# Column sums of the latents' squares moved between the products of chunk 7's dense groups, and the last dense group moved behind the values

## The chip, the cores and the metric

One core of a Trainium2 chip runs the kernel. The metric is the device time of one execution in microseconds (us); 3 runs of the kernel before were timed.

## What is computed

Two layers of a hybrid decoder, for a prompt of 1024 tokens and 8 sequences of 4 new tokens (NT = 1056 tokens in all, width 1024). Each layer projects the normed input with one matrix, runs an mLSTM over chunks and a latent attention (MLA) beside it, joins both in an output projection, and then adds a convolutional feed-forward part and a gated embedding. The part that matters here, cut from the reference:

```python
h = rmsnorm(x, lw['norm_mix'])
z = h @ lw['w_in']
qm, km, vm, om, im, fm, cq, ckv, kr = jnp.split(z, splits, axis=-1)
...
hm, C, n, m = mlstm_chunkwise(qm, km, vm, ig, lf, C0, n0, m0)
hm = rmsnorm(hm.astype(x.dtype), lw['m_norm']).reshape(B, T, M_WIDTH) * jax.nn.sigmoid(om)
lat = jnp.concatenate([rmsnorm(ckv, lw['mla_kv_norm']), rope(kr, pos)], axis=-1)
qa = (rmsnorm(cq, lw['mla_q_norm']) @ lw['mla_w_uq']).reshape(B, T, A_HEADS, A_NOPE + A_ROPE)
```

`rmsnorm` divides by the root of the mean of squares over the latent's width (384 for `cq`, 256 for `ckv`). The sums of these squares, one number per token and latent, are what the change moves.

## The kernel before, in words

The kernel works on transposed tensors: features on the 128 partitions, tokens along the row. A row of 1056 tokens is cut into NC = 3 column chunks of 352. Float32 products are made of three matmuls of rounded halves (`product3`, lines 223 to 225: high x high, high x low, low x high). Each layer is a series of phases; in a phase every engine has its own program, the engines signal one another through semaphores, and a phase ends with a barrier of all engines once its own waits are through.

The phase of the change is `mix_projection` (line 557 on), which runs once per layer. It computes the matrix product with `w_in` as a list of **dense groups**, `GROUPS`. A group is one tile of 128 output features for one column chunk: 8 steps over the input width of 3 matmuls each, 24 matmuls of 128x352, into one PSUM bank. ScalarE evacuates each group (`evacuate`). The last four weight jobs hold 24 groups (`MIXED` and on); these are dealt out to the 8 mLSTM chunks of 128 tokens, three to a chunk, so that they cover the chunk's steps on the other engines. TensorE's loop (line 1035) reads for each chunk c:

```python
dense(MIXED + 3 * c)
spread(c)
dense(MIXED + 3 * c + 1)
scores(c)
dense(MIXED + 3 * c + 2)
values(c)
```

`spread` brings decay rows and the transposed keys to PSUM, VectorE and ScalarE make decay matrices of them (`decays`), `scores` multiplies keys and queries (L988), VectorE multiplies both (`decayed_scores`, L747), and `values` (L1001, L1002, L1008) makes the numerators and the state's update, from which VectorE computes the chunk's heads and the new state (`outputs`). ScalarE squares the heads (`squares`, L886). The last groups are output gates (`og`): ScalarE puts them into one of two buffers `og_staging` (L843), and SyncE stores each to DRAM (`out_gate`, L628). SyncE's list is fixed: behind the last store of a gate comes the store of the final state (L652), and then its waits for every store, which the end of the phase needs.

In chunks 4 to 6 ScalarE squares the latents' tiles and VectorE adds them up (`latent_squares`), into `core.norm` for `cq` and `mem.sqk` (in the profile kv_squares) for `ckv`. After the loop TensorE waits for the last evacuation and makes for each of the two rows of squares 9 column sums: each takes a tile of 128 tokens as stationary operand and a column of ones as moving one (L1046), into a PSUM bank of its own. ScalarE takes the root (L931), VectorE the inverse (L813, the tile `mla_rt`), and TensorE turns the inverses of `cq` into rows with 9 transposes (L1051), in banks 0 to 2. This is the end of the phase. The next one, `mla_prepare`, begins with SyncE's loads (L1122, L1123), VectorE's scaling of `cq` (L1329) and the parts of `cq` that TensorE waits for.

## Time and profile before

| | |
|---|---|
| median of 3 runs | 3104.38 us (3102.88 to 3104.58) |
| the profiled execution's own time | 3111.33 us |
| its span in the profile | 3109.5 us |
| TensorE busy | 96% of the span |
| VectorE busy | 51% |
| ScalarE busy | 36% |
| mean granted clock of TensorE | 0.978 |

The span is what the profile covers of one execution; times in rows are microseconds from its start. The page's first part lists busy shares; the timeline lists instructions in order, with the idle time before one and who ended it. A granted clock of 1.00 is 2.4 GHz, one of 0.50 is 1.2 GHz. Each sum, and each product of the scores and values, is recorded as two passes, so 9 sums appear as 18 matmuls. The transposes are recorded as one.

### The profile page before, as it was taken

Reading aid. Unit: us, or ns where it says so; the run is one execution under the profiler, and the core shown is the slowest. Engines: PE = TensorE matmul, PEld = TensorE weight load, DVE = VectorE, ACT = ScalarE, POOL = GpSimd, SP = SyncE. Lnnn points to the kernel's source line nnn. Section 1 sums busy time; section 2 is a strip of 40 time slices with the busy share of each in tenths; the row PEclk is TensorE's granted clock in tenths of the full one; section 3 lists DMA queues with packets and bytes.
Section 4 is the critical chain, followed back from the end, with each engine's and each line's share of the span. In section 5 each row is a group of like instructions: output and inputs, shape, how many; then the busy total and the mean of one; then the engine's idle time right before and its main releaser. Section 6 shows DMA issues by size and latency. Waiting matters only on the chain. (4 is left out here: it accounts for less than half of the span.)

```text
span 3109.5 us, 46695 instructions
## 1 busy us (share of the span) xinstructions
PE 2984.0 (96%) x19219; PEld 2809.4 (90%) x19219; DVE 1581.0 (51%) x2696; ACT 1134.9 (36%) x2148; POOL 142.8 (5%) x260
## 2 busy tenths in 40 slices
PE   6999989999999999999989999999999999999997
PEld 5998755899999999998989887559999999999997
DVE  5233634565454555457661346445654555445665
ACT  6223423443333323335452333334533223333353
POOL 0000300000000000000000004000000000000000
PEclk9999889999999999999999989999999999999999
DMA  3101243421111111112221021533211111111121
GB/s 129 42 28 45 94 145 113 151 73 55 41 50 47 41 55 41 55 47 82 89 71 42 14 94 57 175 99 137 73 55 41 41 55 43 53 41 41 47 96 70
DMA packets 70742, 215.40 MB, mean 69 GB/s; under 512 B 6522, under 2 KB 43386, under 8 KB 54146
## 3 DMA queue, kind: packets, MB, share of 16 engines
q1 hardware_dynamic: 70530, 212.42, 19.8%
q8 instruction: 152, 2.49, 0.3%
q14 instruction: 60, 0.49, 0.1%
HBM read 193.52 MB, written 18.87 MB: 68 GB/s over the span
## 5 line engine op out<-in xcount | busy, mean ns | idle before, releaser
L223 PE MATMUL psum<-h_chunk,out_weight_parts 128*128 128x352 f32 x2112 | 681.5, 323 | 0.0
L224 PE MATMUL psum<-h_chunk,out_weight_parts 128*128 128x352 f32 x2112 | 677.1, 321 | 0.0
L225 PE MATMUL psum<-h_chunk,out_weight_parts 128*128 128x352 f32 x2112 | 676.4, 320 | 0.0
L2233 DVE SCALAR_TENSOR_TENSOR conv_sum<-u_padded,vectors,conv_sum 128x1024 f32<-128x1024 f32 x176 | 226.3, 1286 | 540.1 <-ACT conv_sum L2085 537.0
L224 PEld LDWEIGHTS psum<-h_chunk,out_weight_parts 128*128 128x128 f32 x2112 | 396.8, 188 | 0.0
L223 PEld LDWEIGHTS psum<-h_chunk,out_weight_parts 128*128 128x128 f32 x2112 | 396.2, 188 | 0.0
L225 PEld LDWEIGHTS psum<-h_chunk,out_weight_parts 128*128 128x128 f32 x2112 | 395.9, 187 | 0.0
L223 PE MATMUL psum<-g_parts,out_weight_parts 128*128 128x352 f32 x960 | 309.3, 322 | 0.0
L224 PE MATMUL psum<-g_parts,out_weight_parts 128*128 128x352 f32 x960 | 309.0, 322 | 0.0
L225 PE MATMUL psum<-g_parts,out_weight_parts 128*128 128x352 f32 x960 | 308.8, 322 | 0.0
L2259 DVE TENSOR_TENSOR x<-x,psum 128x352 f32<-128x352 f32 x528 | 254.9, 520 | 94.4 <-PE psum L225 94.0
L2081 ACT ACTIVATE u_padded<-psum 128x352 f32<-128x352 f32 (+1 forms) x264 | 119.8, 454 | 494.1 <-PE psum L225 494.1
L217 DVE TENSOR_TENSOR out_weight_parts<-out_weight_stage,out_weight_parts 128x2048 fp32r<-128x2048 f32 x80 | 183.3, 2292 | 62.6 <-ACT out_weight_parts L211 62.6
L223 PE MATMUL psum<-h_high,mix_weight_parts 128*128 128x352 f32 x576 | 192.9, 335 | 13.1 <-DVE mix_weight_parts L217 10.1
L2097 ACT ACTIVATE g_parts<-conv_sum 128x1056 fp32r<-128x1056 f32 x40 | 43.4, 1086 | 417.5 <-PE psum L225 345.3
L224 PE MATMUL psum<-h_low,mix_weight_parts 128*128 128x352 f32 x576 | 187.5, 325 | 0.0
L225 PE MATMUL psum<-h_high,mix_weight_parts 128*128 128x352 f32 x576 | 187.4, 325 | 0.0
L225 PEld LDWEIGHTS psum<-g_parts,out_weight_parts 128*128 128x128 f32 x960 | 180.6, 188 | 0.0
L224 PEld LDWEIGHTS psum<-g_parts,out_weight_parts 128*128 128x128 f32 x960 | 180.3, 188 | 0.0
L223 PEld LDWEIGHTS psum<-g_parts,out_weight_parts 128*128 128x128 f32 x960 | 180.3, 188 | 0.0
L2085 ACT ACTIVATE conv_sum<-psum,vectors 128x352 f32<-128x352 f32 x264 | 170.5, 646 | 0.0
L211 ACT ACTIVATE out_weight_parts<-out_weight_stage 128x2048 fp32r<-128x2048 f32 x80 | 152.7, 1908 | 6.1 <-PEq L142 6.0
(356 smaller groups left out, 5502.0 us busy)
## 6 DMA issues: line engine op xcount, KB each, us to landing
out_weight_stage<-w_up_dram SPq DMA_DIRECT2D x44, 1024.0 KB, 4.7
out_weight_stage<-w_down_dram SPq DMA_DIRECT2D x22, 1024.0 KB, 4.7
mix_weight_stage<-w_in_dram SPq DMA_DIRECT2D x18, 1024.0 KB, 4.9
pages<-cache_dram SPq DMA_DIRECT2D x64, 288.0 KB, 4.4
out_weight_stage<-w_out_dram SPq DMA_DIRECT2D x16, 1024.0 KB, 5.9
out_weight_stage<-w_gate_dram SPq DMA_DIRECT2D x16, 1024.0 KB, 4.8
pages<-cache_dram SPq DMA_DIRECT2D x64, 160.0 KB, 2.6
x<-x_in_dram SPq DMA_DIRECT2D x6, 1408.0 KB, 11.1
```

The costliest lines, as they stand in the source:

```text
L211: act.activation(dst[:, 0, 0:width], self.stage[:, staged, 0:width], ACT.Copy).then_inc(self.ph["hi_made"], 1)
L217: dve.tensor_tensor(dst[:, 1, 0:width], self.stage[:, slot % self.stages, 0:width], dst[:, 0, 0:width].bitcast(F32), ALU.subtract).then_in ...
L223: pe.matmul(out, lhs[0], rhs[0], start=first, stop=False)
L224: pe.matmul(out, lhs[0], rhs[1], start=False, stop=False)
L225: return pe.matmul(out, lhs[1], rhs[0], start=False, stop=last)
L2081: act.activation(u[:, q, 2 + c * CH:2 + c * CH + n], src[:, 0:n], ACT.Copy)
L2085: op = act.activation(t[:, q, chunk(c)], src, ACT.Identity, bias=bias, scale=w2)
L2097: act.activation(dst, t[:, 1, :], ACT.Copy).then_inc(ph["ghi_made"], 1)
L2233: dve.scalar_tensor_tensor(t[:, q, 0:SEQ], row[:, tap:tap + SEQ], w, t[:, q, 0:SEQ], ALU.mult, ALU.add).then_inc(ph["conv_step"], 1)
L2259: dve.tensor_tensor(X[:, k, chunk(c)], X[:, k, chunk(c)], ps[:, (6 + n) % 8, 0:CH], ALU.add).then_inc(ph["x_made"], 1)
```

## The change

In chunk 7 the first dense group gets the 9 column sums of `core.norm`, the second those of `mem.sqk`. One sum stands behind each of the first 7 steps of the group, two behind its end. The last dense group moves behind values(7), and waits until the roots are taken, since its bank is the one in which the sums now lie (`SUM_GROUP`, the group that used the bank before). ScalarE takes the roots behind the evacuation of chunk 7's second group, then squares the heads, then evacuates the last group. VectorE makes the inverse ahead of outputs(7). Roots and inverses lie in unused columns of `mem.cwc` instead of a tile of their own. The transposes stay at the end, behind the last evacuation.

```diff
--- before.py
+++ after.py
@@ -608,6 +608,7 @@
         ring = WeightRing(None, ph, "mix_projection", stages=1, stage=mem.mix_stage, parts=mem.mix_parts, ready=ready)
         first_third = 1 if l else 0
         LATE = KX * (2 - first_third)
+        SUM_GROUP = len(GROUPS) - 4
         ps = core.psum
 
         def bank(g):
@@ -806,11 +807,12 @@
                 decayed_scores(c)
                 if 4 <= c < 7:
                     latent_squares(c)
+                if c == NCK - 1:
+                    dve.wait_ge(ph["rt_step"], 2)
+                    dve.reciprocal(mem.rt_inverse, mem.rt).then_inc(ph["rs_made"], 1)
                 outputs(c)
                 if c in (1, 3):
                     ring.lo(dve, 7 + c // 2, JW)
-            dve.wait_ge(ph["rt_step"], 2)
-            dve.reciprocal(mem.rt[:, 1], mem.rt[:, 0]).then_inc(ph["rs_made"], 1)
 
         @block.scalar
         def _(act):
@@ -924,17 +926,19 @@
                 if 4 <= c < 7:
                     latent_squares(c)
                 evacuate(MIXED + 3 * c + 1)
-                evacuate(MIXED + 3 * c + 2)
-                if c == NCK - 1:
-                    for i, d in enumerate((Q_RANK, KV_RANK)):
-                        act.wait_ge(ph["lsum_done"], i + 1)
-                        act.activation(mem.rt[:, 0, i, :], ps[:, i, 0:TT], ACT.Sqrt, bias=core.eps,
-                                       scale=1.0 / d).then_inc(ph["rt_step"], 1)
-                squares(c)
+                if c < NCK - 1:
+                    evacuate(MIXED + 3 * c + 2)
+                    squares(c)
+            for i, d in enumerate((Q_RANK, KV_RANK)):
+                act.wait_ge(ph["lsum_done"], 2)
+                act.activation(mem.rt[:, :, i], ps[:, bank(SUM_GROUP), TT * i:TT * (i + 1)], ACT.Sqrt,
+                               bias=core.eps, scale=1.0 / d).then_inc(ph["rt_step"], 1)
+            squares(NCK - 1)
+            evacuate(len(GROUPS) - 1)
 
         @block.tensor
         def _(pe):
-            def dense(g):
+            def dense(g, latent=None):
                 j, i, kind, t, c = GROUPS[g]
                 if g in START:
                     pe.wait_ge(ph["lo_made"], j + 1 - ready)
@@ -951,7 +955,12 @@
                         w = [W[:, q, k * 256 + i * P:k * 256 + (i + 1) * P] for q in range(2)]
                         x = [H(q, k, chunk(c)) for q in range(2)]
                         mm = product3(pe, ps[:, bank(g), 0:CH], w, x, k == 0, k == KX - 1)
+                    if latent is not None and k < KX - 1:
+                        latent_sum(latent, k)
                 mm.then_inc(ph["mm_done"], 1)
+                if latent is not None:
+                    for c in range(KX - 1, TT):
+                        latent_sum(latent, c)
 
             def gate_columns():
                 pe.wait_ge(ph["gate_act"], 6)
@@ -1008,6 +1017,16 @@
                     mm = pe.matmul(ps[part(h), B_UPD, (h // 2) * DV1:(h // 2 + 1) * DV1],
                                    kw[:, c % 2, h * 64:(h + 1) * 64], vTM[:, c, h, :], start=True, stop=True)
                 mm.then_inc(ph["upd_done"], 1)
+
+            def latent_sum(i, c):
+                if c == 0:
+                    pe.wait_ge(ph["lsq_added"], 2 + i)
+                    pe.wait_ge(ph["bank_free"], SUM_GROUP + 1)
+                n = TT * i + c
+                mm = pe.matmul(ps[:, bank(SUM_GROUP), n:n + 1], (core.norm, mem.sqk)[i][:, token_tile(c)],
+                               core.ones[:, 0:1], start=(n == 0), stop=True, skip_group_check=True)
+                if c == TT - 1:
+                    mm.then_inc(ph["lsum_done"], 1)
 
             if not ready:
                 pe.wait_ge(ph["lo_made"], 1)
@@ -1033,23 +1052,21 @@
             pe.wait_ge(ph["state_zeroed"], 3)
             pe.wait_ge(ph["cwc_made"], 2)
             for c in range(NCK):
-                dense(MIXED + 3 * c)
+                dense(MIXED + 3 * c, 0 if c == NCK - 1 else None)
                 spread(c)
-                dense(MIXED + 3 * c + 1)
+                dense(MIXED + 3 * c + 1, 1 if c == NCK - 1 else None)
                 scores(c)
-                dense(MIXED + 3 * c + 2)
-                values(c)
+                if c < NCK - 1:
+                    dense(MIXED + 3 * c + 2)
+                    values(c)
+            values(NCK - 1)
+            pe.wait_ge(ph["rt_step"], 2)
+            dense(len(GROUPS) - 1)
             pe.wait_ge(ph["bank_free"], len(GROUPS))
-            pe.wait_ge(ph["lsq_added"], 3)
-            for i, squares in enumerate((core.norm, mem.sqk)):
-                for c in range(TT):
-                    mm = pe.matmul(ps[:, i, c:c + 1], squares[:, token_tile(c)], core.ones[:, 0:1],
-                                   start=(c == 0), stop=True, skip_group_check=True)
-                mm.then_inc(ph["lsum_done"], 1)
             pe.wait_ge(ph["rs_made"], 1)
             for c in range(TT):
                 tr = pe.transpose(ps[:, c // 4, c % 4 * P:(c % 4 + 1) * P],
-                                  mem.rt[:, 1, 0, c:c + 1].to_broadcast([P, P]), core.ident)
+                                  mem.rt_inverse[:, c, 0:1].to_broadcast([P, P]), core.ident)
             tr.then_inc(ph["rows_done"], 1)
 
 
@@ -1069,7 +1086,7 @@
     krot = at(M_KROT, "k_rotated", [P, NT])
     cs = at(M_CS, "rope_cos_sin", [P, 2, NT])
     hrt = at(M_KROT + NT, "h_rms", [P, 2, 4 * TT])
-    rt, c0 = mem.rt, mem.c0
+    c0 = mem.c0
     og = at(M_KN, "og_all", [P, 4, NT])
     take = core.slab.bump(M_UQ + 4 * 768, M_CS)
     kw = take("ks_weighted", [NS, 256])
@@ -1207,7 +1224,7 @@
                 for c in range(TT):
                     out = ps[:, RB[1] + c // 4, c % 4 * P:(c % 4 + 1) * P] if c < TT - 1 else \
                         ps[:, TAIL[1][0], TAIL[1][1]:TAIL[1][1] + P]
-                    tr = pe.transpose(out, rt[:, 1, 1, c:c + 1].to_broadcast([P, P]), core.ident)
+                    tr = pe.transpose(out, mem.rt_inverse[:, c, 1:2].to_broadcast([P, P]), core.ident)
                 tr.then_inc(ph["rb_done"], 1)
 
             def numerators():
@@ -2790,7 +2807,6 @@
         self.sqt = at(M_QR + NT, "one_square", [P, NT])
         self.c0 = at(M_KN + 4 * NT, "state_sample", [P, DEC_BATCH, 2, DV1])
         self.uq = at(M_KN + 4 * NT + DEC_BATCH * 2 * DV1, "q_weight_stage", [P, 2, 768])
-        self.rt = at(M_KROT + NT + 72, "mla_rt", [P, 2, 2, TT])
         self.H = Halves(at(M_CATM, "h_high", [P, KX, NT], F32R), at(X_AT, "h_low", [P, KX, NT], F32R))
         self.mix_parts = at(M_KN, "mix_weight_parts", [P, 2, 2, JW], F32R)
         self.mix_stage = at(M_QR, "mix_weight_stage", [P, 1, JW])
@@ -2807,6 +2823,7 @@
         self.vTM = at(M_V, "m_v", [P, TT, M_HEADS, DV1])
         self.rows = at(M_ROWS, "m_rows", [64, NT])
         self.cwc = at(M_CWC, "m_columns", [P, TT, 96])
+        self.rt, self.rt_inverse = self.cwc[:, :, 4:6], self.cwc[:, :, 6:8]
         self.hS = at(M_HS, "m_h_sample", [P, M_HEADS, M_DV])
         self.ssq = at(M_SSQ, "m_ssq", [P, 4 * TT])
```

**TensorE, end of chunk 7's first dense group in layer 0.** L223 to L225 are one step of a group, L971 (L980 after) and L978 (L987 after) are `spread`. Before:

```order
L223 MATMUL psum<-h_high,mix_weight_parts 128x352
L224 MATMUL psum<-h_low,mix_weight_parts 128x352
L225 MATMUL psum<-h_high,mix_weight_parts 128x352
L971 MATMUL psum<-m_rows,constants 128x128 [waits h_made_0]
L971 MATMUL psum<-m_rows,constants 128x128 x7
L978 MATMUL psum<-constants,m_k 128x128 [waits state_made_0]
L978 MATMUL psum<-constants,m_k 128x128
```

With the change (L1026 is a sum; norm holds the squares of `cq`):

```order
L1026 MATMUL psum<-constants,norm 128x1
L223 MATMUL psum<-h_high,mix_weight_parts 128x352
L224 MATMUL psum<-h_low,mix_weight_parts 128x352
L225 MATMUL psum<-h_high,mix_weight_parts 128x352
L1026 MATMUL psum<-constants,norm 128x1 x2
L980 MATMUL psum<-m_rows,constants 128x128 [waits h_made_0]
L980 MATMUL psum<-m_rows,constants 128x128 x7
L987 MATMUL psum<-constants,m_k 128x128 [waits state_made_0]
```

The sums of `cq` stand singly behind the steps, the last two together behind the group. The second group reads in the same way, with kv_squares.

**TensorE, from chunk 7's scores to the end of the phase.** L988 (L997 after) are the scores, L1001, L1002 and L1008 (L1010, L1011 and L1017) the values. Before:

```order
L988 MATMUL psum<-m_q,mix_work 128x128 [waits kT_made_0,sd_made_0]
L988 MATMUL psum<-m_q,mix_work 128x128 x3
L223 MATMUL psum<-h_high,mix_weight_parts 128x352 [waits bank_free_0]
...
L1001 MATMUL psum<-m_v,mix_work 128x129 [waits sd_made_0,state_made_0,qa_made_0,dm_made_0]
L1002 MATMUL psum<-mix_work 128x129
...
L1008 MATMUL psum<-m_v,mix_work 64x129 x3
L1046 MATMUL psum<-constants,norm 128x1 [waits lsq_added_0,bank_free_0]
L1046 MATMUL psum<-constants,norm 128x1 x8
L1046 MATMUL psum<-constants,kv_squares 128x1 x9
L1051 MATMUL psum<-constants,mla_rt 128x128 [waits rs_made_0]
L1051 MATMUL psum<-constants,mla_rt 128x128 x8
```

With the change:

```order
L1026 MATMUL psum<-constants,kv_squares 128x1 x2
L997 MATMUL psum<-m_q,mix_work 128x128 [waits kT_made_0,sd_made_0]
L997 MATMUL psum<-m_q,mix_work 128x128 x3
L1010 MATMUL psum<-m_v,mix_work 128x129 [waits sd_made_0,state_made_0,qa_made_0,dm_made_0]
L1011 MATMUL psum<-mix_work 128x129
...
L1017 MATMUL psum<-m_v,mix_work 64x129 x3
L223 MATMUL psum<-h_high,mix_weight_parts 128x352 [waits bank_free_0,rt_step_0]
L224 MATMUL psum<-h_low,mix_weight_parts 128x352
L225 MATMUL psum<-h_high,mix_weight_parts 128x352
```

The values stand directly behind the scores, the last dense group behind the values and behind a wait for the roots (rt_step), and behind that group only the transposes are left.

**ScalarE, the end of the phase.** L843 (L845 after) evacuates an output gate, L877 (L879) is the decay exponential, L886 (L888) a square of the heads. Before:

```order
L877 ACTIVATE mix_work<-mix_work,m_columns 128x128 x3
L843 ACTIVATE og_staging<-psum 128x352 [waits og_stored_0,mm_done_0]
L843 ACTIVATE og_staging<-psum 128x352 [waits og_stored_1,mm_done_0]
L931 ACT_TABLE_LOAD
L931 ACTIVATE mla_rt<-psum,constants 128x9 [waits lsum_done_0] x2
L886 ACTIVATE mix_work,m_ssq<-m_v 128x128 [waits sq_step_0,h_made_0]
L886 ACTIVATE mix_work,m_ssq<-m_v 128x128 [waits sq_step_0] x3
```

With the change:

```order
L879 ACTIVATE mix_work<-mix_work,m_columns 128x128 x3
L845 ACTIVATE og_staging<-psum 128x352 [waits og_stored_0,mm_done_0]
L934 ACT_TABLE_LOAD
L934 ACTIVATE m_columns<-psum,constants 128x9 [waits lsum_done_0] x2
L888 ACTIVATE mix_work,m_ssq<-m_v 128x128 [waits sq_step_0,h_made_0]
L888 ACTIVATE mix_work,m_ssq<-m_v 128x128 [waits sq_step_0] x3
L845 ACTIVATE og_staging<-psum 128x352 [waits og_stored_1,mm_done_0]
```

The table load and the two roots stand ahead of the last evacuation instead of behind it, and so do the squares of the heads. SyncE's own order is as before: the last gate's store, then the state's.

## Rows read from the trace of the kernel before

**Rows 1.** The page: busy shares, and a group of weight loads (busy us, mean ns).

```profile
PE 2984.0 (96%) x19219; PEld 2809.4 (90%) x19219; DVE 1581.0 (51%) x2696; ACT 1134.9 (36%) x2148; POOL 142.8 (5%) x260
...
L224 PEld LDWEIGHTS psum<-h_chunk,out_weight_parts 128*128 128x128 f32 x2112 | 396.8, 188 | 0.0
```

**Rows 2.** Timeline, layer 0: start, duration, engine, line, operation, idle before.

```profile
303.32 0.72 PE L988 MATMUL psum<-m_q,mix_work 64*128 64x128 f32 x8
303.96 0.43 PE L223 MATMUL psum<-h_high,mix_weight_parts 128*128 128x352 f32 x1
...
307.94 0.39 PE L1001 MATMUL psum<-m_v,mix_work 128*128 128x129 f32 x2
...
311.77 3.28 PE L1046 MATMUL psum<-constants,norm 128*128 128x1 f32 x18
314.92 3.98 PE L1046 MATMUL psum<-constants,kv_squares 128*128 128x1 f32 x18
319.55 2.18 PE L1051 MATMUL psum<-constants,mla_rt 128*128 128x128 f32 x9 [0.66 <-DVE mla_rt L813]
```

**Rows 3.** Timeline, TensorE, layer 1, the same place.

```profile
1842.83 2.17 PE L1046 MATMUL psum<-constants,norm 128*128 128x1 f32 x18
1844.86 3.70 PE L1046 MATMUL psum<-constants,kv_squares 128*128 128x1 f32 x18
1849.22 2.18 PE L1051 MATMUL psum<-constants,mla_rt 128*128 128x128 f32 x9 [0.66 <-DVE mla_rt L813]
```

**Rows 4.** Timeline, ScalarE, layer 0.

```profile
318.93 0.27 ACT L931 ACTIVATE mla_rt<-psum,constants 128x9 f32<-128x9 f32 x1 [3.57 <-PE psum L1046]
...
320.61 0.19 ACT L886 ACTIVATION_READ_ACCUMULATOR mix_work<-m_v 128x1 f32 x1
```

**Rows 5.** Timeline, VectorE, layer 0.

```profile
304.08 0.76 DVE L747 TENSOR_TENSOR mix_work<-psum,mix_work 128x256 f32<-128x256 f32 x2 [3.33 <-PE psum L988]
...
311.96 0.76 DVE L763 TENSOR_TENSOR m_v<-psum,mix_work 128x256 f32<-128x256 f32 x2
...
319.23 0.27 DVE L813 RECIPROCAL mla_rt<-mla_rt 128x18 f32<-128x18 f32 x1 [5.12 <-ACT mla_rt L931]
```

**Rows 6.** Timeline, SyncE's transfers, layer 0, and one of layer 1.

```profile
308.63 0.32 SPq L628 DMA_DIRECT2D out_gate<-og_staging  x1
314.20 0.34 SPq L652 DMA_DIRECT2D state_p_out_dram<-mix_work  x1
322.69 0.33 SPq L1122 DMA_DIRECT2D rope_cos_sin<-cos_sin_dram  x1
323.07 0.43 SPq L1123 DMA_DIRECT2D og_all<-out_gate  x1
...
1852.76 0.33 SPq L1122 DMA_DIRECT2D rope_cos_sin<-cos_sin_dram  x1
```

**Rows 7.** Stretches: length, busy of each engine, granted clock (PEclk), DMA share, GB/s.

```profile
170.00:311.80 141.80, 141.80 (x940) 127.36 (x938) 48.60 (x127) 44.09 (x127) 0.00 (x0) 1.00 0.12 40
...
311.80:313.00 1.20, 1.20 (x12) 1.20 (x10) 1.07 (x5) 0.00 (x0) 0.00 (x0) 0.83 0.00 0
...
329.70:332.80 3.10, 3.08 (x11) 3.10 (x12) 3.10 (x5) 1.75 (x6) 0.54 (x1) 0.50 0.88 373
332.80:336.00 3.20, 3.20 (x21) 3.20 (x21) 2.51 (x7) 1.09 (x2) 1.91 (x3) 0.96 0.09 31
...
1845.00:1846.00 1.00, 1.00 (x7) 1.00 (x7) 0.17 (x1) 0.27 (x1) 0.00 (x0) 0.59 0.00 0
```

**Rows 8.** Timeline, TensorE, three sums between dense groups of the output projection.

```profile
606.38 0.32 PE L225 MATMUL psum<-heads_chunk,out_weight_parts 128*128 128x352 f32 x1
606.54 0.72 PE L2369 MATMUL psum<-constants,norm 128*128 128x1 f32 x6
...
607.37 0.32 PE L224 MATMUL psum<-heads_chunk,out_weight_parts 128*128 128x352 f32 x1
```

**Rows 9.** SyncE's own waits, 285 to 345 us: total, times, longest.

```profile
SPq L657 <- DMA state_p_out_dram<-mix_work: 1.8, 1, 1.8
```

## The prediction

> **What bounds the kernel now.** I read the page first. TensorE is busy for 96% of the span [rows 1], so the time can fall only where TensorE stands still or works slowly. The change touches one such place, the end of the mix projection, which comes once in each of the two layers. I then read TensorE's timeline there. In layer 0 the values of chunk 7 run from 307.94 to 311.77, then come the 18 column sums of squares (two passes each, so 36 matmul records), up to 318.90, a pause, and nine transposes up to 321.73 [rows 2]. In layer 1 the same places are 1842.83 (call the end of the values V), 1848.56 and 1851.40 [rows 3]. ScalarE and VectorE show that the chain is serial: sums, root (318.93), inverse (319.23), transposes (319.55) [rows 2, 4, 5]. SyncE issues its first transfer of the next phase at 322.69 and 1852.76 [rows 6]. So V to the next phase takes 10.92 us in layer 0 and 9.93 in layer 1. That is all that can be won, about 21 us in 3111.33. The difference of 1 us between the layers is the granted clock: it falls to the lower level (0.50, 1.2 GHz) early in the sums of layer 0 and late in those of layer 1 [rows 7].
>
> **The sums, moved between products.** No sum is removed; 36 (two layers of 18) stand elsewhere. The price of one alone between products of a dense group is not in the trace. The nearest place has three sums (six passes) between two dense groups: from the last product before (606.38) to the second after them (607.37) are 0.99 us, where two steps without sums take 0.32 [rows 8]. Thus three sums cost 0.67, one 0.22. The first load of weights of such a piece runs beside the product ahead, and what is then exposed is the second load and that of the next product, again two. I take 0.23 us per sum, 4.14 per layer. The lower bound is the 0.226 of layer 1's sums at the higher clock (2.03 us from 1842.83 to 1844.86 for nine), the upper the 0.41 of the nine that follow (3.70 us) [rows 3].
>
> That a load runs beside the product ahead is shown by the dense products: a load takes 188 ns by its mean [rows 1], yet they start every 0.16 us (606.38 to 606.54) [rows 8]. The Trainium skill (TensorE: Matmul & The Clock Gate, Part 3, The mechanism) says that weight loads overlap matmuls in flight only where the row groups differ, which these full loads do not. By that rule a single sum would expose three loads instead of two (its price is in the rivals). The rows speak against it.
>
> **A wait that appears.** Values(7) now stand directly behind scores(7). Before, the last dense group covered the multiplication of scores and decays on VectorE: the group began at 303.96, VectorE finished at 304.84 [rows 2, 5]. With a handover of 0.05 (319.50 to 319.55, inverse to transposes) TensorE waits 304.89 - 303.96 = 0.93 us. The decay exponentials are long done and cost nothing. What is behind this wait on the queue are values(7) and the last dense group, all of it on the path.
>
> **Edits that cost nothing.** The root moves on ScalarE behind the evacuation of the second dense group; its table load and two roots (0.27 us each) run while TensorE does the values (3.83 us), and the last dense group, which waits for them, comes later. The inverse (0.27 us) stands ahead of outputs(7), which wait for the values anyway. squares(7) start after the heads (312.72, that is 4.8 us behind the start of the values), take 1.6 us (319.20 to 320.80) and end 6.4 behind it; the last evacuation is due 3.83 + 3.98 (303.96 to 307.94) = 7.8 behind it [rows 2, 4, 5]. If that cover were gone, the squares' whole 1.6 us would stand ahead of the last evacuation and on the path. The strided place of the roots concerns 18 elements a row.
>
> **The end of the phase.** The last dense group ends its slots at E = V + 4.14 + 0.93 = V + 5.07. Now its evacuation and its store are late too. Before, the store was issued 0.69 us behind that point (308.63 - 307.94), and the state's store came at 314.20, far ahead of the end [rows 2, 6]. After the change both are queued on SyncE behind the last evacuation: og_staging at E + 0.69, the state 0.38 later (the distance of two issues, 322.69 to 323.07). SyncE must see the state land: 0.34 of issue and 1.8 of waiting [rows 6, 9]. This gives V + 5.07 + 0.69 + 0.38 + 2.14 = **V + 8.28**. TensorE's nine transposes wait for the same evacuation, start with the store's issue at about E + 0.7 and take 2.18 us even at the lower clock, so they end at V + 7.95 or earlier: **the state's landing is late next**, by 0.3 us at least. Before, the transposes, the phase's last work, ended at V + 9.96 (321.73) in layer 0 and V + 8.57 in layer 1. So 1.68 us and 0.29 us are won, 1.97 in all, if the clock stays up as before until V. The change may then bring 3111.33 - 1.97 = 3109.4 on the profiled execution, and 3102.4 on the median of the runs, which is 6.95 us below that execution; I make the sum on the difference and subtract it from the median.
>
> **The clock.** What the clock did before: behind the last dense product it stayed at 1.00 through the 3.83 us of the values alone of every chunk (its mean is 1.00 over 170.00 to 311.80, which holds all eight), but with sums behind the values it fell 4.7 us behind the end of the dense group (307.94) in layer 0 (inside 311.80 to 313.00, whose mean is 0.83, so at about 312.6) and 6.2 us behind it (V - 3.83 = 1839.00) in layer 1 (0.59 in 1845.00 to 1846.00, so about 1845.2), though TensorE was busy for 1.00 of that time [rows 7]. After the change the stretch without dense products between the second and the third dense group is two trailing sums 0.46, scores 0.64 (303.32 to 303.96), the wait 0.93 and the values 3.83 [rows 2]: 5.86 us. That lies between 4.7 and 6.2, and is emptier than the values alone. **I expect the clock to fall there in at least one of the layers.** It then stays low through the rest of the values and part of the last dense group. The price is bounded from below by the dense products at the lower clock at the next phase's start: 11 in the 3.10 us from 329.70, all at 0.50, where 0.16 each would be 1.8, a loss of 1.3 us [rows 7]. From above: the whole of the values (slower by the same 0.41/0.226 as the sums, 3.1 us more) and the whole last group (24 x 0.12 = 2.9), 6.0 us. As a fall can come anywhere in the values, I take 2.7 us, nearer the lower end because the clock was back at once after those 3.1 us of dense work (0.96 in the next 3.2), and 1.5 falls over the two layers: 4.0 us.
>
> The Trainium skill (TensorE: Matmul & The Clock Gate, table in "Why this matters for your kernels") warns of idle gaps between bursts of matmuls. By that rule nothing would happen here, since the engine idles for under 1 us, and the result would be that of the first rival. The rows of the sums, a fall at full busy time, say that idling is not needed.
>
> **Forecast: 3104.38 - 1.97 + 4.0 = 3106.4 us**, the likeliest case, chance 0.62; its own range is one fall at the low price to two falls at a higher one, 3103.8 to 3110. A measurement here can tell 0.2%, 6.2 us, from no change; so this is "no change".
>
> **Rivals.**
> - The clock holds in both layers: 3102.4 us. For it speaks that all chunks of the layer hold through their values [rows 7]; against it the 5.86 us. Chance 0.18.
> - The sums are dear when single. If their first load did not run beside the product ahead, three passes of 0.113 would be exposed, 0.34 us, and the two layers would lose 18 x 0.11 x 2 = 4.0 us: 3106.4 with the clock held; at the upper bound of 0.41 they lose 6.5, 3108.9. For it speaks that every piece changes between the two kinds of matmul; against it the 0.67 for three [rows 8]. Chance 0.07. This is the rule on row groups cited above.
> - **Slower than before by over 0.2%**: the clock falls right behind the scores and, with too little work in the slow values, does not come back until the last dense group is over, in both layers. At 6.0 us each this is 3102.4 + 12.0 = 3114.4. It decides for slower from 4.1 us per layer on (6.2 + 1.97 over two). Against it: the clock came back after 3.1 us of dense work. Chance 0.08.
> - The landing does not bind and the transposes run at the higher clock (twice as fast, 2.18 becomes 1.1): the phase ends at V + 6.9, 1.4 us earlier per layer, 3099.6 us. It needs a store that lands sooner than its like before. Chance 0.05.
> - That the change does not do what it says would be a wait of the first sum for squares or for the bank. The squares' additions end in chunk 6, and the bank was evacuated behind values(6), before the group starts: no wait, within the 0.05 above.
>
> **Range and chances.** The range takes the forecast's own, the clock held and dear sums: 3101.5 to 3110.5, and leaves out the two ends, under 0.15. Faster by over 0.2% (below 3098.2) has no mechanism here: 0.02. Slower by over 0.2%: the third rival and the tail of the first case, 0.09. Within: 0.89.
>
> **What would show it.** Single sums between products at steps of about 0.23 us; TensorE idle 0.9 us between scores and values for VectorE; the granted clock below 1.00 inside the last values and products of 0.29 us in the last group; SyncE's wait for state_p_out as the end of the phase, 8.3 us plus the fall's price behind the old V. The forecast is wrong if the clock is at 1.00 until the transposes, or if the steps at the sums are well above 0.3 us, or if the next phase starts later behind the landing than the 0.96 and 1.36 us that lay between the transposes and SyncE's first issue.

## The result, and the profile after

The change made the kernel slower: 3121.81 us (median of 5 runs, 3112.66 to 3124.23) against 3104.58 us before (5 runs in turn with them, 3102.88 to 3107.24). The ratio on record is 1.0049, with a 95% interval of 1.0039 to 1.006. The ratios in this document are those of the record, which aren't quotients of the medians (here 1.0055), and they leave out three executions of 5584, 5999 and 12777 us, of blocks_old_order, dummy_blocks and the kernel before. The result is outside the predicted range, and it is the sign of the third rival. The runs also lie wider apart than before, over 11.6 us instead of 4.4.

The profiled execution is the quickest of the five: 3112.66 us, span 3110.9 us. The page looks as before, with the same busy time of TensorE to 0.4 us [rows 1] and the same weight loads. (The profiled execution of before, 3111.33 us, was slower than all its timed runs; a second profile of it, below, has a span of 3099.7.)

```profile
PE 2984.4 (96%) x19219; PEld 2810.4 (90%) x19219; DVE 1580.2 (51%) x2696; ACT 1134.8 (36%) x2148; POOL 142.8 (5%) x260
...
L224 PEld LDWEIGHTS psum<-h_chunk,out_weight_parts 128*128 128x128 f32 x2112 | 396.8, 188 | 0.0
```

A busy share cannot show this change, because an engine at half its clock is as busy as one at full clock. The timeline does. TensorE in layer 0, the kernel after, in the order of time; these rows answer to [rows 2]:

```profile
293.55 0.32 PE L225 MATMUL psum<-h_high,mix_weight_parts 128*128 128x352 f32 x1
293.70 0.28 PE L1026 MATMUL psum<-constants,norm 128*128 128x1 f32 x2
293.84 0.41 PE L223 MATMUL psum<-h_high,mix_weight_parts 128*128 128x352 f32 x1
...
294.40 0.28 PE L1026 MATMUL psum<-constants,norm 128*128 128x1 f32 x2
...
302.22 0.42 PE L1026 MATMUL psum<-constants,kv_squares 128*128 128x1 f32 x2
...
303.53 0.42 PE L1026 MATMUL psum<-constants,kv_squares 128*128 128x1 f32 x2
...
309.53 1.22 PE L997 MATMUL psum<-m_q,mix_work 64*128 64x128 f32 x8
311.81 0.55 PE L1010 MATMUL psum<-m_v,mix_work 128*128 128x129 f32 x1 [1.06 <-DVE mix_work L748]
...
318.65 0.66 PE L223 MATMUL psum<-h_high,mix_weight_parts 128*128 128x352 f32 x1
...
324.40 1.20 PE L1068 MATMUL psum<-constants,m_columns 128*128 128x128 f32 x9 [0.55 <-ACT og_staging L845]
```

In the first group a step of three products and one sum takes 0.70 us (293.70 to 294.40), where a step without a sum takes 0.48: 0.22 for a sum. In the second group the same step takes 1.31 us (302.22 to 303.53). The wait for VectorE is there (1.06). The scores take 1.22 instead of 0.72, the values 311.81 to 318.65, which is 6.84 us instead of 3.83.

Stretches of the same place (length, busy of each engine, granted clock, DMA share, GB/s):

```profile
293.00:297.70 4.70, 4.70 (x37) 4.69 (x35) 0.99 (x3) 1.61 (x9) 0.00 (x0) 1.00 0.01 3
297.70:299.40 1.70, 1.70 (x18) 1.58 (x18) 0.58 (x1) 0.16 (x1) 0.00 (x0) 1.00 0.29 106
299.40:300.40 1.00, 1.00 (x8) 1.00 (x9) 0.94 (x4) 0.66 (x3) 0.00 (x0) 1.00 0.00 0
300.40:301.40 1.00, 1.00 (x6) 1.00 (x6) 0.51 (x2) 0.89 (x4) 0.00 (x0) 0.55 0.00 0
301.40:309.50 8.10, 8.10 (x32) 8.10 (x32) 0.00 (x0) 0.49 (x2) 0.00 (x0) 0.50 0.00 0
309.50:318.60 9.10, 8.04 (x33) 5.66 (x33) 1.44 (x6) 1.69 (x3) 0.00 (x0) 0.50 0.06 20
318.60:321.00 2.40, 2.40 (x10) 2.35 (x9) 2.06 (x6) 1.28 (x7) 0.00 (x0) 0.50 0.00 0
321.00:323.80 2.80, 2.80 (x18) 2.54 (x16) 0.00 (x1) 0.33 (x2) 0.00 (x0) 1.00 0.02 6
```

The clock falls at about 300.5, inside the second dense group, 1 us behind its start, and comes back at about 321, 2.3 us into the last dense group, which has no sums in it. Before, this whole place was at 1.00 up to 311.80 [rows 7]. TensorE was busy for all of the 7.4 us of these rows ahead of the fall. What it did there was the end of the first group with single sums, the two sums behind it, the spread (8 products of four rows, recorded as 16), the transposed keys, and one step of the second group.

In layer 1 the clock fell later, inside the values:

```profile
1836.00:1842.80 6.80, 5.74 (x44) 5.21 (x42) 1.02 (x3) 2.18 (x4) 0.00 (x0) 1.00 0.08 27
1842.80:1843.90 1.10, 1.10 (x6) 0.74 (x5) 0.00 (x0) 0.00 (x0) 0.00 (x0) 0.74 0.00 0
1843.90:1849.60 5.70, 5.70 (x23) 4.68 (x23) 2.57 (x9) 1.40 (x7) 0.00 (x0) 0.50 0.00 0
1849.60:1850.70 1.10, 1.10 (x7) 1.10 (x7) 0.00 (x0) 0.21 (x2) 0.00 (x0) 0.74 0.00 0
```

The end of the phase is that of the prediction. SyncE's transfers in layer 0, then in layer 1, which answer to [rows 6]:

```profile
324.37 0.32 SPq L629 DMA_DIRECT2D out_gate<-og_staging  x1
324.80 0.37 SPq L653 DMA_DIRECT2D state_p_out_dram<-mix_work  x1
328.12 0.33 SPq L1139 DMA_DIRECT2D rope_cos_sin<-cos_sin_dram  x1
...
1853.58 0.36 SPq L653 DMA_DIRECT2D state_p_out_dram<-mix_work  x1
1857.38 0.33 SPq L1139 DMA_DIRECT2D rope_cos_sin<-cos_sin_dram  x1
```

**Where the time went.** I measure each layer from the start of chunk 7's first dense group, in us, to the end of the values, to SyncE's first issue of the next phase, and to the first dense product of the next phase. Two profiles of each kernel:

| | values end, L0 / L1 | next SyncE issue, L0 / L1 | next dense product, L0 / L1 | span |
|---|---|---|---|---|
| before | 18.48 / 18.48 | 29.33 / 28.34 | 36.36 / 35.01 | 3109.5 |
| before, second | 18.48 / 18.49 | 27.29 / 28.30 | 34.32 / 34.97 | 3099.7 |
| after | 27.01 / 21.08 | 36.40 / 31.26 | 43.43 / 37.94 | 3110.9 |
| after, second | 22.54 / 28.33 | 32.33 / 38.20 | 39.36 / 44.87 | 3114.5 |

Against the second profile of before, the last dense columns of the two layers together are 12.1 and 14.9 us later, and the spans 11.2 and 14.8 us longer. So in the profiles of the change the loss is in these two places, within 1 us. The first profile of before is longer mostly for another reason: its clock was low for 140.0 us in all, in the second for 122.6, mostly in stretches that this change doesn't touch; 2.0 us of the difference lie in layer 0's place.

### The profile page after: what moved, and what is told of

It is laid out like the page before. It is cut to its first block and busy times, and to the rows that moved or that the text cites. A ratio compares the mean times of both kernels' runs of the same rounds, so it can differ in the third digit from the quotient of the medians.

```text
span 3110.9 us, 46701 instructions
## 1 busy us (share of the span) xinstructions
PE 2984.4 (96%) x19219; PEld 2810.4 (90%) x19219; DVE 1580.2 (51%) x2696; ACT 1134.8 (36%) x2148; POOL 142.8 (5%) x260
## 5 line engine op out<-in xcount | busy, mean ns | idle before, releaser
L223 PE MATMUL psum<-h_chunk,out_weight_parts 128*128 128x352 f32 x2112 | 681.5, 323 | 0.0
L225 PE MATMUL psum<-h_chunk,out_weight_parts 128*128 128x352 f32 x2112 | 676.4, 320 | 0.0
L223 PEld LDWEIGHTS psum<-h_chunk,out_weight_parts 128*128 128x128 f32 x2112 | 396.2, 188 | 0.0
L225 PEld LDWEIGHTS psum<-h_chunk,out_weight_parts 128*128 128x128 f32 x2112 | 395.8, 187 | 0.0
L223 PE MATMUL psum<-g_parts,out_weight_parts 128*128 128x352 f32 x960 | 309.3, 322 | 0.0
L225 PE MATMUL psum<-g_parts,out_weight_parts 128*128 128x352 f32 x960 | 308.8, 322 | 0.0
L223 PE MATMUL psum<-h_high,mix_weight_parts 128*128 128x352 f32 x576 | 198.2, 344 | 13.1 <-DVE mix_weight_parts L217 10.1
L225 PE MATMUL psum<-h_high,mix_weight_parts 128*128 128x352 f32 x576 | 189.7, 329 | 0.0
L225 PEld LDWEIGHTS psum<-g_parts,out_weight_parts 128*128 128x128 f32 x960 | 180.6, 188 | 0.0
L224 PEld LDWEIGHTS psum<-g_parts,out_weight_parts 128*128 128x128 f32 x960 | 180.4, 188 | 0.0
L223 PEld LDWEIGHTS psum<-g_parts,out_weight_parts 128*128 128x128 f32 x960 | 180.3, 188 | 0.0
```

The source lines that it names most:

```text
L223: pe.matmul(out, lhs[0], rhs[0], start=first, stop=False)
L224: pe.matmul(out, lhs[0], rhs[1], start=False, stop=False)
L225: return pe.matmul(out, lhs[1], rhs[0], start=False, stop=last)
```

## The experiments

Two theories were set against each other at the start. S: the single sums between the products bring the clock down inside the dense groups, and keep it down. L (the theory of the prediction): the stretch of scores, wait and values without dense work brings it down. Each expectation is quoted as it stood before the run.

### The two halves of the change, apart

**single_old_order** keeps the single sums and puts the last dense group back ahead of the values (squares and last evacuation change places again, the sums lie in a free bank).

```diff
                 scores(c)
-                if c < NCK - 1:
-                    dense(MIXED + 3 * c + 2)
-                    values(c)
-            values(NCK - 1)
-            pe.wait_ge(ph["rt_step"], 2)
-            dense(len(GROUPS) - 1)
+                dense(MIXED + 3 * c + 2)
+                values(c)
```

> The sums stand singly between the products as in the change, but the last dense group is back ahead of the values (the sums lie in a free part of another bank). Theory S (single sums between products bring the granted clock down inside the dense groups and keep it down): 3110 to 3125 us, the clock at 0.50 inside chunk 7's first or second group. Theory L (the stretch without dense products behind the second group, scores, wait and values, brings it down): the stretch is gone, so 3101 to 3106 us and 1.00 through the groups and the values.

**group_moved_only** is the other half: the kernel before, with its last dense group behind the values and all sums at the end.

```diff
-                dense(MIXED + 3 * c + 2)
+                if c < NCK - 1:
+                    dense(MIXED + 3 * c + 2)
                 values(c)
+            dense(len(GROUPS) - 1)
```

> The kernel before with nothing but the last dense group moved behind the values (squares of the heads ahead of its evacuation); the sums stay at the end. The wait for VectorE, 0.93 us per layer, comes in, nothing goes. Theory S: 3105 to 3108 us. Theory L: the stretch of scores, wait and values (5.4 us) brings the clock down before the last group: 3109 to 3120 us.

**blocks_new_order** is the change with the nine sums in a block behind their group; **blocks_old_order** does the same to single_old_order.

```diff
-                    if latent is not None and k < KX - 1:
-                        latent_sum(latent, k)
                 mm.then_inc(ph["mm_done"], 1)
                 if latent is not None:
-                    for c in range(KX - 1, TT):
+                    for c in range(TT):
                         latent_sum(latent, c)
```

> The order of the change, but each nine sums stand as one block behind their dense group, none between products. Theory S: 3101 to 3108 us, since nothing disturbs the groups. Theory L: the stretch without dense products is even longer (2.0 us of sums, scores, wait, values), so 3112 to 3125 us.

> Sums as blocks behind the first and the second dense group of chunk 7, last dense group ahead of the values as before, root and inverse hidden beside them. Both theories: no fall before the values end, so the same or a little below the kernel before, 3100 to 3105 us. If it is slow, sums anywhere ahead of the values cost the clock.

Measured, with 3104.81 us for the kernel before (24 runs on the same chip); the last column is the next phase's first SyncE issue, measured as in the table above:

| kernel | median us | ratio, 95% interval | L0 / L1 |
|---|---|---|---|
| single_old_order | 3113.09 | 1.0024 (1.0013 to 1.0035) | 29.26 / 28.45 |
| blocks_old_order | 3112.98 | 1.0019 (1.0009 to 1.0028) | 30.98 / 29.66 |
| group_moved_only | 3111.58 | 1.002 (1.0011 to 1.0029) | 30.07 / 31.69 |
| blocks_new_order | 3117.1 | 1.0034 (1.0021 to 1.0048) | 32.70 / 35.11 |

Each half alone costs 7 to 8 us, and together they cost 12 to 17: the loss is no single fault of either. Both theories missed at blocks_old_order, where both expected no loss, and S as first worded, on single sums alone, missed at blocks_new_order too (3117.1 for at most 3108) and at group_moved_only (3111.58 for at most 3108). L missed at single_old_order; its ranges for group_moved_only and blocks_new_order were met.

Not all of these losses lie at the place of the change. Against the second profile of before, the next dense product of the two layers together comes 2.1 us later in single_old_order, 5.0 in blocks_old_order, 6.2 in group_moved_only and 12.2 in blocks_new_order, while the spans are longer by 7.1, 9.0, 9.5 and 13.7 us. That profile of before is itself one of the quicker executions, 3.3 us below its median. The 1.5 to 5 us outside the two layers' places are not explained.

The stretches of single_old_order, layer 0 and then layer 1, show what decides:

```profile
299.60:302.90 3.30, 3.30 (x14) 3.30 (x14) 1.18 (x4) 1.54 (x5) 0.00 (x0) 0.51 0.00 0
303.50:319.00 15.50, 13.04 (x91) 11.52 (x90) 3.59 (x12) 4.26 (x13) 0.00 (x0) 1.00 0.09 31
...
1828.00:1848.00 20.00, 16.83 (x123) 15.18 (x121) 5.62 (x17) 5.80 (x18) 0.00 (x0) 1.00 0.10 34
```

In layer 0 the clock fell at the same point as in the kernel after (at the start of the second group), without any moved group: L alone can't be it. In layer 1 the same program held 1.00 up to the end of the values, and there the next dense product came at 35.13 against 35.01 before. So **in this layer, where the clock held, the sums ahead of the values were neither a gain nor a loss**; they only traded places. (The values end 3.7 us later, at 22.21, and the next phase's first issue comes at 28.45 against 28.34: behind the values the landing of the state's store is late next.)

Blocks don't prevent the fall. In blocks_old_order it came in both layers within 1.2 us of the start of the second group, which has no sum between its products, and the clock was back after 3 to 4 us. Layer 1:

```profile
1830.00:1833.00 3.00, 3.00 (x12) 3.00 (x12) 1.38 (x5) 1.55 (x5) 0.00 (x0) 0.50 0.00 0
1834.00:1849.00 15.00, 13.10 (x94) 11.58 (x92) 3.59 (x12) 4.26 (x13) 0.00 (x0) 1.00 0.07 24
```

The stretches of group_moved_only in layer 0 show the other theory's part, the wait and then a full clock up to the sums. Its timeline row comes first:

```profile
305.23 0.46 PE L1004 MATMUL psum<-m_v,mix_work 128*128 128x129 f32 x2 [1.06 <-DVE mix_work L747]
```

```profile
304.00:315.00 11.00, 9.39 (x63) 7.81 (x59) 3.32 (x11) 3.31 (x11) 0.00 (x0) 1.00 0.08 29
316.50:335.00 18.50, 15.26 (x62) 13.23 (x62) 11.16 (x19) 7.66 (x13) 1.86 (x2) 0.50 0.50 198
```

In layer 1 of the same execution the clock was low from 1838 to 1845, from within the values on, and the state's store was issued at 23.72 against 20.74 in layer 0. So the fall that the prediction feared does come without any sum in the groups, in one layer of two, and costs 3.0 us. L exists; by itself it is small.

### What a single sum does to the clock, measured by itself

**dummy_single** is the kernel before with 252 column sums more, of a constant into an unused column: 18 for each of the chunks 0 to 6 of both layers, placed as the change places them in chunk 7. **dummy_blocks** has the same 252 in blocks of nine behind each of the two groups. The real computation is whole in both.

```diff
                         mm = product3(pe, ps[:, bank(g), 0:CH], w, x, k == 0, k == KX - 1)
+                    if dummy and k < KX - 1:
+                        dummy_sum()
                 mm.then_inc(ph["mm_done"], 1)
+                if dummy:
+                    for _ in range(TT - KX + 1):
+                        dummy_sum()
```

> The kernel before with extra column sums of the identity, singly between the steps of the first two dense groups of chunks 0 to 6 (7 times 18 a layer, 252 in all), their results unused. As TensorE's work alone they cost 252 x 0.23 = 58 us, so 3163 us with the clock up. Theory S (behind such a mixture the clock falls at the next thin stretch and, at the lower clock, the groups with single sums do not bring it back): well above that, 3200 us or more, with stretches at 0.50 of 10 us and longer in the mix projection. Theory L (only the stretch of scores, wait and values matters): 3163 us and 1.00 in the chunks.

> The same 252 extra sums as nine behind each of those groups, none between products. TensorE's work alone is the same, 3163 us. Theory S: falls at the blocks (sums and spread together are 3.9 us without dense products), each over after one stretch of dense products, some 1.5 us per fall and up to two per chunk: 3175 to 3200 us, less than with single sums. Theory L: 3163 us.

Measured: 3217.65 us (ratio 1.0348, 1.0317 to 1.0378) for the single ones and 3184.17 us (1.0261, 1.0242 to 1.028) for the blocks, with 3103.0 for the kernel before. I estimate the sums' own work at 252 x 0.23 = 58 us. The rest, 57 us single and 23 us in blocks, I put down to the clock. The stretches, dummy_single first:

```profile
172.50:188.50 16.00, 16.00 (x65) 15.76 (x64) 1.97 (x6) 2.01 (x6) 0.00 (x0) 0.50 0.06 24
190.00:202.00 12.00, 12.00 (x87) 10.72 (x86) 3.16 (x10) 2.54 (x10) 0.00 (x0) 1.00 0.00 0
203.00:216.00 13.00, 13.00 (x55) 12.76 (x54) 1.25 (x4) 1.34 (x4) 0.00 (x0) 0.50 0.01 1
```

The same place of dummy_blocks:

```profile
168.00:171.00 3.00, 3.00 (x28) 2.87 (x28) 1.07 (x3) 0.25 (x1) 0.00 (x0) 1.00 0.82 259
171.60:174.80 3.20, 3.20 (x13) 3.20 (x12) 0.42 (x1) 0.70 (x3) 0.00 (x0) 0.54 0.01 5
176.00:195.00 19.00, 19.00 (x140) 17.58 (x139) 4.73 (x14) 3.52 (x13) 0.00 (x0) 1.00 0.00 1
```

Both fall at 171 to 172, at the end of the spread and of the first group's sums, at a busy time of 1.00. In blocks the clock is back after 3 to 4 us of plain dense work, and this repeats once a chunk: 171 to 175, 195 to 198, 219 to 222, 243 to 246. Once more in each layer it fell elsewhere; in layer 0 that was at 202, behind the second block of nine and inside the scores, with no spread near. With single sums it stays low until the group without sums comes (at 184.6) and is back 4 us later; the falls between the chunks of the phase last 13 to 17 us, all but one of 7. In all the clock was low for 289.6 us of the span against 180.4, and for 122.6 and 140.0 in the kernel before. So two things are shown. The added sums, together with the spread or the scores behind them, bring the clock down, single or not. And with a sum in every step, a group at the low clock mostly doesn't bring it back, while one without sums did within 5 us each time. Not always: in single_old_order (above) and in layer 0 of the second profile of after (300 to 304) it came back inside a group with single sums. No run has the sums with dense products on both sides and nothing small near, so what they would do alone isn't shown.

### The change once more

> The changed kernel once more, for a second profile. If the place of the falls is chance (theory S, a fall anywhere from the first block of thin work on), the low stretches lie elsewhere than in the first profile, and the place costs between 1 and 10 us a layer more than before.

Measured: 3116.26 us (3 runs), ratio 1.0044 (1.003 to 1.0059). This time layer 0 came off lightly (low from 300 to 304 and from 311 to 317), and layer 1 fell at 1829.6, in the spread, 1.0 us ahead of the second group:

```profile
1827.00:1830.00 3.00, 3.00 (x28) 2.97 (x26) 0.52 (x1) 0.46 (x1) 0.00 (x0) 0.93 0.16 60
1830.60:1852.60 22.00, 20.94 (x83) 18.51 (x82) 4.29 (x15) 4.66 (x14) 0.00 (x0) 0.50 0.02 8
```

The long fall isn't bound to a layer; which of the falls one gets changes from one execution to the next. That is probably why the runs of the kernel after spread so much.

### Without the wait at the values

**wait_filled** fills TensorE's wait for VectorE with six dense products into a bank that is read out already (their result is not used).

```diff
+            pe.wait_ge(ph["bank_free"], len(GROUPS) - 2)
+            for _ in range(6):
+                pe.matmul(ps[:, bank(len(GROUPS) - 3), 0:CH], ring.parts[:, 0, 0, 0:P], H(0, 0, chunk(0)),
+                          start=True, stop=True)
             values(NCK - 1)
```

> The changed kernel with six dense products (128x352, 0.97 us, results unused) between chunk 7's scores and its values, where TensorE waits about 1 us for VectorE anyway. They cost nothing as work. If the stretch of scores, wait and values is what brings the clock down (theory L), it is now broken and the time comes down to 3106 us or less. If the falls come from the single sums and the stretches around spread (theory S), this helps only the falls behind the scores: 3112 to 3118 us, still slower than the kernel with the old order of the groups.

Measured: 3116.54 us, ratio 1.004 (1.0026 to 1.0055), no better than the change. The stretches show why:

```profile
301.80:314.40 12.60, 12.60 (x54) 12.36 (x53) 1.74 (x6) 3.40 (x9) 0.00 (x0) 0.50 0.04 14
1834.60:1857.80 23.20, 23.20 (x90) 20.81 (x91) 4.82 (x16) 4.97 (x16) 0.00 (x0) 0.50 0.03 8
```

In both layers the clock was low before the filled place was reached. In layer 0 it came back at about 315, right behind the six products, and the values then ran at full speed; in layer 1 it did not. TensorE's busy time is the whole of both stretches: no idle time at all is needed to stay at the low clock. At that clock the six products are not free either: from the start of the scores to the values it is 3.08 us here and 2.28 in the kernel after, both in layer 0. So this run shows that the wait isn't needed for the loss, but not what the change would cost without it.

### Two other ways to shorten the end

**broadcast_sums** takes the kernel before and replaces the sums of `cq` and their transposes by three products with a matrix of ones, which give each sum on all rows at once; root and inverse are then taken over 128x1024 numbers in PSUM.

```diff
+            dve.reciprocal(ps[:, 0:2, :], ps[:, 0:2, :])
+            dve.reciprocal(ps[:, 2, P - NS:P], ps[:, 2, P - NS:P])
...
+            for out, at, n in ((ps[:, 0, :], 0, 512), (ps[:, 1, :], 512, 512), (ps[:, 2, P - NS:P], SEQ, NS)):
+                mm = pe.matmul(out, core.ones, core.norm[:, at:at + n], start=True, stop=True)
```

> The kernel before with the sums of cq made by a stationary block of ones and the squares as moving operand (1056 columns, two passes), so that every partition gets them and the nine transposes go; root and inverse in place; the nine column sums of ckv run beside them. By both theories nothing is ahead of the values, so no fall there; the phase then ends with the state's landing, V + 6.3 us instead of V + 10.9 and V + 9.9: 3.6 to 4.6 us less per layer, 3095 to 3098 us.

A miss: 3109.26 us, ratio 1.0016 (1.0007 to 1.0025). TensorE's part went as thought, 2.12 us for the products instead of the sums and transposes, but the chain is now VectorE's (timeline):

```profile
310.41 2.12 PE L1050 MATMUL psum<-norm,constants 128*128 128x512 f32 x6
...
312.57 1.27 ACT L934 ACTIVATE psum<-psum,constants 128x1024 f32<-128x1024 f32 x2 [4.03 <-PE psum L1050]
...
313.87 6.57 DVE L813 RECIPROCAL psum<-psum 128x1024 f32<-128x1024 f32 x1 [1.12 <-ACT psum L934]
```

The inverse takes 6.57 us, where another operation of VectorE on 128x1024 numbers takes 1.28 (the scaling of `cq`, 322.29). The expectation, which let the phase end with the state's landing at V + 6.3, left no room for it.

**tail_reordered** moves nothing ahead of the values. It changes the order of the end alone: nine sums of `cq`, three of `ckv` as cover for root and inverse, the transposes, and the other six sums beside them.

```diff
+            latent_sums(0, range(TT))
+            latent_sums(1, range(3))
             pe.wait_ge(ph["rs_made"], 1)
...
             tr.then_inc(ph["rows_done"], 1)
+            latent_sums(1, range(3, TT))
```

> The kernel before with only its tail changed: behind the values come the nine sums of cq, three of ckv, the transposes, and the other six of ckv; each latent has its own root and inverse, and the heads' squares stand between the roots. Nothing moves ahead of the values, so by theory S no fall comes in. The pause of 0.65 us goes, and root, inverse and transposes of cq lie beside the sums of ckv's; the transposes end at V + 4 to V + 5 and the phase ends behind the last sums, V + 6.5 to V + 8.5 instead of V + 8.6 to V + 10: 1.5 to 2 us less per layer, 3100 to 3102 us.

Measured: 3102.0 us against 3104.77, ratio 0.9992 (0.9983 to 1.0001); the interval just takes in 1, so a gain isn't shown. It is the only version at or below the kernel before. The timeline of its end, layer 0:

```profile
309.93 2.17 PE L1050 MATMUL psum<-constants,norm 128*128 128x1 f32 x18
311.96 0.81 PE L1050 MATMUL psum<-constants,kv_squares 128*128 128x1 f32 x6
312.71 1.87 PE L1059 MATMUL psum<-constants,mla_rt 128*128 128x128 f32 x9
314.37 2.56 PE L1050 MATMUL psum<-constants,kv_squares 128*128 128x1 f32 x12
```

The transposes start 2.8 us behind the values in both layers instead of 5.7 to 7.8, and the next phase's first issue is at 26.93 and 27.45, against 27.29 to 29.33 and 28.3 before. The clock falls at 313, as in the kernel before (stretches):

```profile
293.00:313.00 20.00, 20.00 (x142) 18.15 (x141) 6.36 (x20) 6.19 (x20) 0.00 (x0) 1.00 0.08 28
313.60:329.80 16.20, 13.42 (x55) 11.79 (x54) 11.40 (x19) 8.05 (x15) 2.04 (x2) 0.50 0.58 227
```

**before_again** is the kernel before, unchanged, for a second profile.

> The kernel before once more, for a second profile: the same 3102 to 3109 us. If falls of the clock outside the place of the change are chance, their places and number differ from the first profile, while the place of the change costs the same within 2 us.

Measured: 3101.46 us, span 3099.7, just below the expected 3102 to 3109. Its places stand in the first table: layer 1's is the same as before, layer 0's 2.0 us shorter, since the clock fell 3.1 us behind the values and not 0.8. This row of its timeline, layer 0, bears on the prediction's gain:

```profile
315.93 2.18 PE L1051 MATMUL psum<-constants,mla_rt 128*128 128x128 f32 x9 [0.66 <-DVE mla_rt L813]
```

## Why the prediction was wrong

**The sums' price: right.** Predicted 0.23 us each, measured 0.22 in the first group of layer 0. In layer 1, with the clock at 1.00 up to the scores' end, the 18 sums put that end at 14.41 us instead of 10.60 behind the first group's start: 3.81 us, 0.21 each, for 4.14 predicted. The rival of dear single sums is out; this also agrees with the rows and not with the rule on row groups of the Trainium skill (TensorE: Matmul & The Clock Gate, Part 3, The mechanism) that was weighed there. That section also lets loads into a background weight buffer run ahead, which the prediction passed over.

**The wait: right.** 1.06 us for 0.93, in both layers.

**The end of the phase: right in kind.** In both profiles of after, the landing of the state's store ends the phase, not the transposes, which at 1.00 take 1.20 us. From its issue to the next phase's first issue there are 3.32 and 3.80 us (first profile); the prediction's 2.14 for the landing and 0.96 or 1.36 behind it make 3.10 and 3.50.

**The gain of 1.97 us: not there.** It was read from one profile, in which the clock fell early in layer 0's sums. In the second profile of before the transposes end at V + 7.92 in layer 0 (315.93 + 2.18, with V = 310.19) and at V + 8.52 in layer 1. Against these the predicted V + 8.28 loses 0.36 us and wins 0.24. So even with the clock up until V, hardly anything could be won, as layer 1 of single_old_order also suggests.

**A fall in the values: right in place and size, for one layer.** Layer 1 of the first profile is the forecast's own case. Its values take 5.5 us instead of 3.83 and its last group about 1.3 more, 3.1 in all for the 2.7 of the prediction, and the next phase begins at 31.26; the prediction's steps give 28.34 - 0.29 + 2.7 = 30.75. The separate run of the moved group has the same fall at 3.0 us.

**The step that failed** is the one ahead of it: that the clock "stays up as before until V", and with it that a fall could come only in the stretch between the second and the third group. I counted the sums ahead of that stretch as work alone, and a dense group with a sum in every step as dense work. In the sum it is the term of 4.0 us for the clock, 1.5 falls at 2.7. What is shown instead: the clock falls at or within 1 us of the start of the second group in layer 0 of the first profile, in both layers of wait_filled and in both layers of after_again; in three of these five places the fall lasted through the values. The price of such a fall in layer 0 of the first profile, against its length at full clock: second group 10.07 us instead of 5.9 (3.98 and nine sums at 0.21), scores 0.5 more, values 3.0 more, last group 1.1 more, together 8.8 us instead of 2.7. The term was 8.8 + 3.1 = 11.9 us in this profile and not 4.0. The steps then give 3104.38 - 1.97 + 11.9 = 3114.3, and 3116.3 without the gain; the medians were 3121.81 and 3116.26.

**The slower rival** had the right sign and nearly that sum (3114.4), but not the place: it let the clock fall behind the scores, at 6.0 us in each layer. That its sum is near is luck. I gave it 0.08 because "the clock came back after 3.1 us of dense work" [rows 7]. That row holds for plain dense work, and again does so in dummy_blocks; it said nothing of a group with sums in it. What should have warned me is in [rows 7] too: there the clock fell at a busy time of 1.00 while TensorE did nothing but these very sums, and the change puts two of them directly ahead of the spread, whose products are small too (four rows). The Trainium skill's warning (TensorE: Matmul & The Clock Gate, "Why this matters for your kernels") is of idle gaps; the falls at the second group came without one.

What stays open: the exact condition under which the clock falls or comes back. The same program at the same point held it in one layer and lost it in the other (single_old_order), so I can say what makes a fall likely, not when it comes. Nor do two profiles settle how the 5.5 us between 3116.3 and the median of 3121.81 are made up; the second profile of after has, in layer 0, a fall of 3 to 4 us and one in the values, and a long one in layer 1, 14.9 us in all.

## What to carry to other kernels

Work moved into a dense stretch of matmuls is not paid by its own time alone: small products spread through dense groups can cost TensorE's clock, and then every matmul around them is slower too (here a step with its sum took 1.31 us instead of 0.70). Keep small work in one block at the end of the dense work, where little is left to slow down, and shorten its chain there; judge such a change by the granted clock of stretches, since busy time doesn't show it. When a profile has shown the clock come back, note behind what kind of work it did.

## What was not expected of the hardware

- The clock fell to the lower level at a busy time of 1.00, with no idle time ahead of it, and stayed there for 23.2 us at a busy time of 1.00 (wait_filled, layer 1).
- With a one-column sum behind every three dense products, the clock took 13 to 17 us to come back to 1.00 in 10 falls of 11 (dummy_single); with plain dense groups 3 to 4 us (dummy_blocks), all but one fall. The number of sums was the same, and the kernels differ by 33 us.
- VectorE's inverse of 128x1024 numbers in PSUM takes 6.57 us, five times its scaling of `cq`, of the same size (1.28).
- Nine transposes of 128x128 take 1.20 us at 1.00, and 2.18 at the lower clock [rows 2].
